# A layer's input modulated and split by ScalarE and VectorE in turn, with two weight quarters split ahead of it

## The reference, cut to what matters

```python
shift1, scale1, gate1, shift2, scale2, gate2 = modulation(cvec, p['w_ada'], p['b_ada'])
h = rms_norm(x, p['norm1_w']) * (1 + scale1) + shift1
(mq, mk, mv, mo, mg, ..., sz, sxbc, sdt, gpre) = split_cols(h @ p['w_in'])
...
x = x + gate1 * (mixed @ p['w_out'])
h2 = rms_norm(x, p['norm2_w']) * (1 + scale2) + shift2
x = x + gate2 * expert_choice_ffn(h2, p['w_router'], p['w_gate'], p['w_up'], p['w_down'])
```

## Time and profile before

| | us |
|---|---|
| median of 3 runs | 2158.97 (2154.82 to 2162.4) |
| profiled execution, device time | 2164.85 |
| its span | 2163.0 |
| PE busy | 1818.3 (84%) |
| DVE busy | 670.4 (31%) |
| ACT busy | 546.1 (25%) |
| POOL busy | 455.3 (21%) |

### The profile page before, as it was taken

How to read it: one execution, slowest core, us unless ns; L and a number is a source line. 1 busy time by engine, 2 the same in 40 slices (tenths; PEclk the granted TensorE clock), 3 DMA queues, 4 the chain that set the end, 5 groups by cost and what they waited for, 6 DMA issues and landing times.

```text
span 2163.0 us, 21993 instructions
## 1 busy us (share of the span) xinstructions
PE 1818.3 (84%) x9096; PEld 1166.2 (54%) x9096; DVE 670.4 (31%) x1239; ACT 546.1 (25%) x1054; POOL 455.3 (21%) x234
## 2 busy tenths in 40 slices
PE   5996988987989888888879969889787997888787
PEld 2885877876743222222258768778685432222233
DVE  2065435558420000011143362446583100101011
ACT  4432343222242111011144323333114211101111
POOL 0655422315310000000035452223262000000000
PEclk8998987979989999999989979889698999999999
DMA  9435233324689999999963433323244699999996
GB/s 356 110 100 216 100 134 110 121 81 156 225 342 393 427 428 426 427 427 427 424 174 129 164 110 135 139 97 140 103 167 188 259 428 426 427 427 428 426 425 278
DMA packets 123539, 567.73 MB, mean 262 GB/s; under 512 B 21808, under 2 KB 31280, under 8 KB 98352
## 3 DMA queue, kind: packets, MB, share of 16 engines
q1 hardware_dynamic: 112656, 543.91, 63.4%
q10 hardware_dynamic: 9920, 20.84, 2.7%
q0 software_dynamic: 864, 1.58, 0.3%
HBM read 550.57 MB, written 15.73 MB: 262 GB/s over the span
## 4 chain that ended last, share of the span: by engine, by line
PE 42%; DMA 35%; DVE 15%; ACT 3%; POOL 2%; issue 1%; SPq 1%; ACTq 0%; DVEq 0%
PE banks L751 19%; PE banks L1250 10%; DMA work<-in_w_gate 7%; DMA ring<-in_w_up 6%; DMA work<-in_w_up 6%; DMA ring<-in_w_down 6%; DMA ring<-in_w_gate 4%; DMA work<-in_w_down 3%; PE banks L1068 2%; DVE work L1783 2%; DMA ring<-in_w_in 2%; POOL small L697 1%; DMA ring<-in_w_branch 1%; DMA ring<-in_w_ada 1%; PE banks L757 1%
## 5 line engine op out<-in xcount | busy, mean ns | idle before, releaser
L683 POOL TENSOR_TENSOR ring_fp32r<-ring,ring_fp32r 128x1024 fp32r<-128x1024 f32 (+1 forms) x164 | 364.3, 2234 | 943.0 <-ACT ring_fp32r L1349 942.9
L1250 PE MATMUL banks<-ring,work 128*64 128x512 f32 x1776 | 402.7, 597 | 77.1 <-DMA ring<-in_w_gate 32.2
L751 PE MATMUL banks<-xT_fp32r,ring_fp32r 128*128 128x384 f32 x1280 | 366.9, 361 | 35.4 <-POOL ring_fp32r L683 32.2
L1349 ACT ACTIVATE work<-banks 32x512 f32<-32x512 f32 (+6 forms) x404 | 205.3, 528 | 456.5 <-PE banks L1250 251.8
L1250 PEld LDWEIGHTS banks<-ring,work 128*64 128x64 f32 x1776 | 122.5, 137 | 335.6 <-issue 199.0
L751 PEld LDWEIGHTS banks<-xT_fp32r,ring_fp32r 128*128 128x128 f32 x1280 | 250.0, 202 | 47.9 <-issue 38.2
L1250 PE MATMUL banks<-work 128*64 128x512 f32 x972 | 225.8, 601 | 40.4 <-DMA work<-in_w_gate 15.1
L751 PE MATMUL banks<-hT_fp32r,ring_fp32r 128*128 128x384 f32 x640 | 225.0, 351 | 0.0
L1349 ACT ACTIVATE ring_fp32r<-ring 128x1024 fp32r<-128x1024 f32 (+1 forms) x164 | 156.3, 971 | 223.7 <-PE banks L751 157.6
L2205 DVE SCALAR_TENSOR_TENSOR xT<-banks,mod,xT 128x128 f32<-128x128 f32 (+1 forms) x128 | 47.1, 413 | 447.2 <-PE banks L1286 446.8
L1250 PEld LDWEIGHTS banks<-work 128*64 128x64 f32 x972 | 67.5, 137 | 180.8 <-issue 112.5
(11 more groups left out here) (283 smaller groups left out, 1787.7 us busy)
## 6 DMA issues: line engine op xcount, KB each, us to landing
ring<-in_w_up SPq DMA_DIRECT2D x38, 2048.0 KB, 30.6
ring<-in_w_gate SPq DMA_DIRECT2D x37, 2048.0 KB, 30.5
ring<-in_w_down SPq DMA_DIRECT2D x36, 2048.0 KB, 30.2
ring<-in_w_in SPq DMA_DIRECT2D x28, 2048.0 KB, 10.1
ring<-in_w_ada SPq DMA_DIRECT2D x24, 2048.0 KB, 8.8
work<-in_w_down SPq DMA_DIRECT2D x20, 2048.0 KB, 30.5
work<-in_w_gate SPq DMA_DIRECT2D x18, 2048.0 KB, 30.5
work<-in_w_up SPq DMA_DIRECT2D x16, 2048.0 KB, 30.6
```

The lines of the kernel that those rows point to most:

```text
L683: ins = pool.tensor_tensor(rounded(w), w, rounded(hi), ALU.subtract)
L751: mm = pe.matmul(dst, a_, b_, start=(first and i == 0), stop=(last and i == 2))
L1250: mm = pe.matmul(dst[64 * hf:64 * hf + 64, :], x(k), w[kk][:, 512 * hf:512 * hf + 512], start=(k == 0), stop=(k == KC - 1), tile_position= ...
L1349: return act.activation(dst, src, ACT.Copy, scale=scale)
```

## The change

- ACT modulates the even chunks alone and copies their high parts to `xT` itself (`modulate_even`); the copy of a chunk stands behind the modulation of the next even one. POOL still subtracts their low parts.
- DVE modulates the odd chunks with TENSOR_SCALAR instructions (two column scalars, multiply and add; `modulate_odd`), and copies and subtracts them as before. It no longer copies even chunks.
- In both layers two weight quarters are split ahead of the input instead of one in layer 1 and none in layer 0, on ACT (`high_parts(2)`) and on POOL (`low_parts(2)`).
- In layer 0 DVE takes the reciprocal and scales the chunks (`modulated(0)`) ahead of the modulation vectors (`adaptive`). In layer 1 the order is small columns, vectors, reciprocal.
- ACT's high part of the small columns (`small_high`) goes ahead of the root in layer 1.
- ACT now waits for `x_moved` ahead of its first modulation. Semaphores are renumbered; `c_ready` is replaced by a step of `dve_step`.

```diff
                 low = [0]
-                if l:
-                    low_parts(1)
+                low_parts(2)
                 for k in range(0, KC, 2):
-                    pool.wait_ge(sem["xh_ready"], 8 * l + k + 1)
+                    pool.wait_ge(sem["xh_ready"], 4 * l + k // 2 + 1)
                     pool.tensor_tensor(rounded(hT[:, k, :]), hT[:, k, :], rounded(HH_IN[:, k, :]), ALU.subtract).then_inc(sem["hl_ready"], 1)
                 low_parts(Q_GATE + 4)
...
+            def modulate_even(layer):
+
+                act.wait_ge(sem["amp_ready"], layer + 1)
+                act.wait_ge(sem["x_moved"], 32 * layer + 16)
+                modulate(layer, 0, 0)
+                for k in range(0, KC, 2):
+                    if k + 2 < KC:
+                        modulate(layer, 0, k + 2)
+                    act.wait_ge(sem["h_ready"], 12 * layer + k // 2 + 1)
+                    copy(rounded(HH_IN[:, k, :]), hT[:, k, :]).then_inc(sem["xh_ready"], 1)
...
             ada_early(0, 0)
             ada_early(0, 2)
+            small_high(0)
             for l in range(L):
...
-                act.wait_ge(par_in[1], 80 * (l + 1))
-                copy(rounded(WSMH), wsm[:, :, :]).then_inc(sem["wsm_hi"], 1)
-                if l:
-                    high_parts(1)
-                modulate(l, 0)
+                high_parts(2)
+                modulate_even(l)
                 high_parts(4)
...
+                    small_high(l + 1)
                     root(l + 1, 0)
...
-                dve.wait_ge(sem["wsm_hi"], l + 1)
-                TTo(rounded(wsm[:, :, :]), wsm[:, :, :], rounded(WSMH), ALU.subtract).then_inc(sem["wsm_lo"], 1)
-
-                modulated(0)
+                if l == 0:
+                    modulated(0)
+                    adaptive()
+                    small_low()
+                else:
+                    small_low()
+                    adaptive()
+                    modulated(0)
 
                 dve.wait_ge(sem["x_moved"], 32 * l + 16)
-                for k in range(KC):
-                    dve.wait_ge(sem["h_ready"], 16 * l + k + 1)
-                    dve.tensor_copy(rounded(HH_IN[:, k, :]), hT[:, k, :]).then_inc(sem["xh_ready"], 1)
-                    if k % 2:
-                        dve.wait_ge(sem["xh_ready"], 8 * l + k + 1)
-                        TTo(rounded(hT[:, k, :]), hT[:, k, :], rounded(HH_IN[:, k, :]), ALU.subtract).then_inc(sem["hl_odd"], 1)
+                done = {}
+
+                def modulate_odd(k):
+                    for g, (a, b) in enumerate(((0, 128), (128, 384))):
+                        ins = TS(hT[:, k, a:b], hT[:, k, a:b], amp[:, 0, k, g:g + 1], mod[:, k, g:g + 1], ALU.mult, ALU.add)
+                    ins.then_inc(dve_step, 1)
+                    done[k] = step()
+
+                modulate_odd(1)
+                for k in range(1, KC, 2):
+                    if k + 2 < KC:
+                        modulate_odd(k + 2)
+                    dve.wait_ge(dve_step, done[k])
+                    dve.tensor_copy(rounded(HH_IN[:, k, :]), hT[:, k, :]).then_inc(dve_step, 1)
+                    dve.wait_ge(dve_step, step())
+                    TTo(rounded(hT[:, k, :]), hT[:, k, :], rounded(HH_IN[:, k, :]), ALU.subtract).then_inc(sem["hl_odd"], 1)
```

More of the change, by code:

```diff
@@ L794, in _ @@
             pe.wait_ge(sem["xT_evac"], 6)
-            pe.wait_ge(sem["c_ready"], 1)
+            pe.wait_ge(dve_step, 3)
             for i in (0, 2):
@@ L1371, in root, with modulate @@
                 act.activation(RSTD, PS[:, 6, 0:T], ACT.Sqrt, scale=1.0 / D, bias=K("eps")).then_inc(sem["rms_ready"], 1)
-            def modulate(layer, which):
-                for k in range(KC):
-                    act.wait_ge(sem["hx_ready"], 16 * layer + 8 * which + k + 1)
-                    for g, (a, b) in enumerate(((0, 128), (128, 384))):
-                        ins = act.activation(hT[:, k, a:b], hT[:, k, a:b], ACT.Identity, scale=amp[:, which, k, g:g + 1],
-                                             bias=mod[:, 24 * which + k, g:g + 1])
-                    ins.then_inc(sem["h_ready"], 1)
+            def modulate(layer, which, k):
+                act.wait_ge(sem["hx_ready"], 16 * layer + 8 * which + k + 1)
+                for g, (a, b) in enumerate(((0, 128), (128, 384))):
+                    ins = act.activation(hT[:, k, a:b], hT[:, k, a:b], ACT.Identity, scale=amp[:, which, k, g:g + 1],
+                                         bias=mod[:, 24 * which + k, g:g + 1])
+                ins.then_inc(sem["h_ready"], 1)
+            def modulate_even(layer):
[7 more added lines that the diff above has]
+                    copy(rounded(HH_IN[:, k, :]), hT[:, k, :]).then_inc(sem["xh_ready"], 1)
             def ada_early(layer, i):
@@ L1388, in ada_early, with small_high @@
                     copy(mod[:, 4 * j:4 * j + 4, :], PS[:, j % 2, 0:8].rearrange("p (a b) -> p a b", a=4)).then_inc(sem["ada_taken"], 1)
+            def small_high(layer):
+                act.wait_ge(par_in[1], 80 * (layer + 1))
+                copy(rounded(WSMH), wsm[:, :, :]).then_inc(sem["wsm_hi"], 1)
             for k in range(KC):
@@ L1608, in _ @@
                     ada_early(l + 1, 0)
-                modulate(l, 1)
+                for k in range(KC):
+                    modulate(l, 1, k)
                 for t in range(TT):
@@ L1726, in modulated, with adaptive @@
                     dve.wait_ge(sem["hx_ready"], 16 * l + 8 * (which + 1))
-                dve.wait_ge(sem["wsm_hi"], l + 1)
-                TTo(rounded(wsm[:, :, :]), wsm[:, :, :], rounded(WSMH), ALU.subtract).then_inc(sem["wsm_lo"], 1)
-                modulated(0)
-                dve.wait_ge(sem["x_moved"], 32 * l + 16)
-                for k in range(KC):
-                    dve.wait_ge(sem["h_ready"], 16 * l + k + 1)
-                    dve.tensor_copy(rounded(HH_IN[:, k, :]), hT[:, k, :]).then_inc(sem["xh_ready"], 1)
-                    if k % 2:
-                        dve.wait_ge(sem["xh_ready"], 8 * l + k + 1)
-                        TTo(rounded(hT[:, k, :]), hT[:, k, :], rounded(HH_IN[:, k, :]), ALU.subtract).then_inc(sem["hl_odd"], 1)
+                def adaptive():
+                    dve.wait_ge(par_in[1], 80 * (l + 1))
+                    dve.wait_ge(sem["ada_taken"], EARLY * (l + 1))
+                    TTo(mod[:, 0:16, :], mod[:, 0:16, :], over(CP("b_ada")[:, 0:16], 2, 2), ALU.add).then_inc(dve_step, 1)
+                    dve.wait_ge(dve_step, step())
+                    STT(amp[:, 0, :, :], mod[:, 8:16, :], 1.0, over(CP("norm1"), 2, 2), ALU.add, ALU.mult).then_inc(sem["amp_ready"], 1)
+                    dve.wait_ge(sem["amp_ready"], l + 1)
@@ new lines, in small_low @@
+                def small_low():
+                    dve.wait_ge(sem["wsm_hi"], l + 1)
+                    TTo(rounded(wsm[:, :, :]), wsm[:, :, :], rounded(WSMH), ALU.subtract).then_inc(sem["wsm_lo"], 1)
+                if l == 0:
[6 more added lines that the diff above has]
+                    modulated(0)
+                dve.wait_ge(sem["x_moved"], 32 * l + 16)
```

13 lines of the change are left out of this document (3 added, 10 removed).

## The result

| | us |
|---|---|
| the change, median of 20 runs | 2175.26 (2163.67 to 2194.26) |
| before, median of 20 runs | 2165.44 (2154.82 to 2179.24) |
| ratio | 1.0054, 95% interval 1.0032 to 1.0076 |
| forecast | 2168.5, range 2156.5 to 2174 |
| profiled execution of the change, device time (span) | 2191.53 (2189.7) |

The change is slower by 11.7 us by the ratio (6.9 to 16.5), 9.8 by the medians, where +9.6 was forecast. The median lies 1.3 above the range. The kernel before has a median of 2165.44 over 20 runs, 6.5 above that of the three runs that the forecast stood on. The profiled execution is the second longest of its 20, so the traces are read by stretches and not by their spans.

What follows compares the result with a forecast made beforehand. No single engine bounds the whole; PE, DMA and DVE hold it together, and each layer's first quarter matmul was watched. Layer 0's +0.4 and layer 1's +9.2 make +9.6 on 2158.97: 2168.5, range 2156.5 to 2174.

Steps and rivals of the forecast that it cites:

- +9.6: Sum of the two layer starts, +0.4 in layer 0 and +9.2 in layer 1.
- The base: Whole kernel before: median of 2158.97, to which the sum was added for 2168.5; its profiled execution took 2164.85.
- DVE and POOL take turns by the instruction: Layer starts: one engine works at a time, alternating when both have work; layer 1's POOL passes add 7.7 between DVE's instructions.
- The pair of TENSOR_SCALARs: Layer 1, DVE's odd chunks: two TENSOR_SCALARs per chunk take 0.60, between bounds of 0.48 and 0.96.
- The clock's 1.1: Layer 1: half-clock matmuls falling on quarters cost 0 to 2.6, taken as 1.1.
- PE's small matmuls start at 52.1 and are dense: Layer 0: first quarter matmul then at 57.6 to 58.9 against 58.08, -0.5 to +0.8, taken as +0.4.
- The wait of ACT: Layer 0: ACT stands some 3 us until 44.6 for the weight tile ahead of its first quarter.
- I count every microsecond at a layer's start as one at the end: Both layers: a shift of the first quarter matmul shifts what follows by as much.
- the halves work as meant: Rival: POOL doesn't break DVE's short instructions in layer 1, PE is fed by even chunks alone; 2156.5, chance 0.17.
- only the chunks collide: Rival: layer 1's quarters 2 and 3 fall behind DVE's last chunk; +4.9, 2164, chance 0.15.
- DVE gets no turn through passes in a row: Rival: layer 1's odd chunks begin only after quarter 3; +12 with the clock, 2171, chance 0.10.

Runs made afterwards that it cites:

- the hold: POOL waits for DVE's second branch product before splitting the next quarters' low parts; on the kernel before 2156.42 (0.9932), on the change 2163.84 (0.9983).

## Why the forecast was right and wrong

**The base.** This is the step that failed, and it carries the miss: "against the median of 2158.97 it is 2168.5". That median was of three runs and the profiled execution lay 5.9 above it; over 20 runs the median is 2165.44, beside the profiled 2164.85. The term was 6.5 too small; 2165.44 and the same +9.6 make 2175.0, against 2175.26 measured. The forecast's other figure, 2174.4 from the profiled execution, is 0.9 under the measured median, while the profiled execution of the change itself took 2191.53. The sum was put on the smaller sample of two, and the range around it was made of mechanisms only, with nothing for the base, though the three runs alone spread over 7.6 us.

**The +9.6.** That it came out so near (9.8 by the medians, 11.7 by the ratio) is in part luck. The start of layer 1 was sized up to 1.3 too high, that of layer 0 some 2 too low in two traces of four, as said below, and the mixers between, which were put at nothing, differ by up to 11 between two traces of the same kernel. The interval of the ratio, 5 either way, doesn't tell a sum of 8 from one of 12.

**DVE and POOL take turns by the instruction.** Right, and shown by the run with the late quarters held: CASTs of 2.49 beside POOL, 0.35 without. The small matmul was to come 1.0 later and came 0.8 later; the last odd chunk was to end 23.0 behind the root and ended 22.2 behind; the first quarter matmul was to be 8.1 later before the clock and 9.2 with it. It was 7.9 and 8.5 later in the two traces of the change against the 15.7 of before's first trace (8.2 and 8.8 against the 15.4 of its second), and 9.2 and 9.4 in those with the hold.

**The pair of TENSOR_SCALARs** was taken as 0.60 between 0.48 and 0.96, and is 0.66. The Trainium skill's cycle table (VectorE: DVE Perf Modes, The TRN2 errata) gave an estimate of 0.32; the trace disagrees, with twice that. For four chunks that is 0.2 more than forecast.

**The clock's 1.1.** The quarters of layer 1 begin at the upper level in all four traces of the change, with and without the hold (matmuls of 0.34 from 1137.50 in the profiled one), so nothing fell on them there. The small matmuls took the lower level until 1135.6. It is in layer 0 that quarters met it: in two of the four traces the first five matmuls of the quarters come 0.32 apart instead of 0.17, some 0.8 in all.

**Layer 0, "PE's small matmuls start at 52.1 and are dense".** Wrong in two traces of four. In the profiled one they started at 51.4 and weren't dense, since DVE's odd chunks were starved as in layer 1. The forecast had counted turns in layer 1 and left them out here but for 0.5 on one chunk. Its end, 57.6 to 58.9, is met in one trace, where the vectors came at 41.4, and two odd chunks were through and the third under way before POOL's passes began (DVE, POOL, PE of the second run of the change with the hold):
```profile
44.73 0.56 DVE L1775 TENSOR_TENSOR hT_fp32r<-hT,xT_fp32r 128x384 fp32r<-128x384 f32 x1
...
46.17 2.58 DVE L1775 TENSOR_TENSOR hT_fp32r<-hT,xT_fp32r 128x384 fp32r<-128x384 f32 x1
48.68 2.50 DVE L1773 CAST xT_fp32r<-hT 128x384 fp32r<-128x384 f32 x1
...
45.61 5.35 POOL L683 TENSOR_TENSOR ring_fp32r<-ring,ring_fp32r 128x1024 fp32r<-128x1024 f32 x2 [45.16 <-ACT ring_fp32r L1349]
...
57.85 0.35 PE L751 MATMUL banks<-xT_fp32r,ring_fp32r 128*128 128x384 f32 x1
```
In the other three traces of the change, with and without the hold, the vectors end at 43.1 to 43.5, and the first quarter matmul is at 59.4, 62.0 and 62.2. In the second trace of the change (59.4) the small matmuls start at 52.7 and are dense, though the vectors end at 43.5: there POOL's first pass comes at 46.4, 3.0 behind the vectors, instead of 2.3 behind them as in the two traces at 62. Before, the first quarter matmul is 16.4 behind the vectors in all five traces with that start; in the change it is 15.9, 16.4, 18.8 and 19.0. The term is thus -0.5 to +2.6 where +0.4 stood. The profiled execution of before, with vectors at 41.7, was one end of the scatter, and it had been read as the kernel's own time. The wait of ACT is there, 1.5 instead of some 3, for the same reason.

**"I count every microsecond at a layer's start as one at the end."** Right on average for delays (10.2 gave 7.8, 5.1 gave 8.7, with intervals of 4 to 5 either way), but not a rule one can add up to a microsecond: the race at the branches takes 4 to 7 of layer 0 or leaves them, and stretches with the same matmuls differ by 6 to 7 with the time at the lower clock.

**The rivals.** The first one's sum has a slip: 1.8 and 0.3 off 2158.97 make 2156.9 and not 2156.5, which changes nothing. That the halves work as meant and that only the chunks collide fell with the trace of the change: quarters 2 and 3 run from 1126.83 to 1131.5, before the first odd chunk is done. That DVE gets no turn through passes in a row did not happen to the chunks, whose instructions got theirs at some 2.5 us each, but it happens, eight passes long, at a place that neither the change nor the forecast spoke of. The earlier trace rows had shown it, and the forecast asked only whether it would occur in the chunks.

## What to carry to other kernels

Where two engines hold each other up as DVE and POOL do here, order their queues as if they were one: what counts is which long instruction of the one stands between the short ones of the other, and a wait of 1.3 us a layer, put into the engine with the long passes, gained 15. When a part that surely starts sooner leaves the time unchanged, list the instructions that take ten times their usual length, in several traces of one kernel, and compare the time at the lower clock up to the same instruction, before doubting the part. A forecast's base wants its own uncertainty, since the difference can be right and the number not.

## What the runs showed of the hardware

A VectorE product of two SBUF tiles can be held through all that GpSimd has in a row. In the 24 cases of the traces without the hold (two layers each), one of the two products was held so in 21. A second product that started between 0.29 us ahead of and 0.09 behind the first of the eight passes took 10.57 to 10.95 (13 cases). A first product that started 0.06 or 0.07 behind the issue of GpSimd's store, with the passes next in its queue, took 11.4 (8 cases); a ninth that started 0.07 behind it took 0.96. A second product that started 0.15 (twice) or 0.27 behind the first pass was held for that pass only, 1.93 to 1.98, and turns followed. With the hold, first products that started 0.06 or 0.07 behind the same issue took 0.96 (7 cases), so it is the passes and not the issue that hold one. The product of the earlier trace rows took 10.5 behind four passes of 2.3 in every trace.

The Trainium skill has whoever issues first block the other for the whole instruction (SBUF — State Buffer, Who interferes with whom). The traces agree for one instruction, as in the turns at the odd chunks; the held product goes beyond it, since in 16 of the 21 cases it had started ahead of the first pass and was still held by what came after. What decides no run here shows.

RECIPROCAL kept its own length beside a pass (2.55 at 1114.02, with POOL at work from 1114.93; 2.54 with nothing on POOL, at 41.99 in the trace of before), while CAST, TENSOR_SCALAR and TENSOR_TENSOR were all held.
